# Reading the moving operand of every split product as two interleaved halves of its columns

## The reference

```python
z = h @ w_in[l]
u = causal_dwconv(h @ w_up[l], ffn_conv_w[l], ffn_conv_b[l])
x = x + (jax.nn.silu(gate) * val) @ w_down[l]
mix = (gate_a * y_a + gate_b * y_b) @ w_out[l]
gu = xb @ w_gu + b_gu
return ((up + 1.0) * glu) @ w_dn + b_dn
```

## Time and profile before

| what | value |
|---|---|
| median of three runs | 3237.35 us |
| the profiled execution's own time | 3235.76 us |
| its span, first to last instruction | 3233.9 us |
| TensorE matmul busy | 3073.2 us, 95% |
| VectorE, ScalarE, GpSimd busy | 59%, 53%, 23% |
| mean granted TensorE clock | 0.969 of full |
| DMA over the span | 677.48 MB, mean 209 GB/s |

### The profile page before, as it was taken

How to read it: one execution, slowest core, us unless ns; L and a number is a source line. 1 busy time by engine, 2 the same in 40 slices (tenths; PEclk the granted TensorE clock), 3 DMA queues, 4 the chain that set the end, 5 groups by cost and what they waited for, 6 DMA issues and landing times. The chain is left out here.

```text
span 3233.9 us, 40774 instructions
## 1 busy us (share of the span) xinstructions
PE 3073.2 (95%) x14356; PEld 2474.9 (77%) x14356; DVE 1923.7 (59%) x2190; ACT 1702.2 (53%) x2270; POOL 751.7 (23%) x409
## 2 busy tenths in 40 slices
PE   7988999998999999989999898999999999999987
PEld 6755778877877787768888776888888888888853
DVE  3247533343376604360032547999999999999973
ACT  4334534333566523332231425877887887887752
POOL 2400144442433243324444330000000000000020
PEclk9987999999999999989999998999999999999998
DMA  4236022222221222212222718999999999999960
GB/s 152 104 137 254 27 78 104 104 79 104 79 74 57 79 91 79 105 52 89 93 104 104 289 61 320 406 410 401 406 407 407 401 407 407 403 406 408 401 257 37
DMA packets 93434, 677.48 MB, mean 209 GB/s; under 512 B 10048, under 2 KB 10432, under 8 KB 32800
## 3 DMA queue, kind: packets, MB, share of 16 engines
q1 hardware_dynamic: 82320, 634.33, 50.2%
q0 software_dynamic: 6912, 25.17, 2.0%
q10 hardware_dynamic: 4112, 16.78, 1.3%
HBM read 637.97 MB, written 38.27 MB: 209 GB/s over the span
## 5 line engine op out<-in xcount | busy, mean ns | idle before, releaser
L143 POOL TENSOR_TENSOR ring_low<-ring,mix_ring_high 128x1024 fp32r<-128x1024 f32 x120 | 291.9, 2468 | 455.3 <-ACT mix_ring_high L138 455.3
L227 PE MATMUL psum<-mix_high,mix_ring_high 128*128 128x512 f32 x864 | 343.1, 397 | 13.1 <-DVE h_low L521 8.6
L229 PE MATMUL psum<-mix_high,ring_low 128*128 128x512 f32 x864 | 337.2, 390 | 0.0
L228 PE MATMUL psum<-h_low,mix_ring_high 128*128 128x512 f32 x736 | 287.4, 391 | 0.0
L143 POOL TENSOR_TENSOR ring_low<-ring,ff_ring_high 128x1024 fp32r<-128x1024 f32 x72 | 175.0, 2462 | 401.5 <-ACT ff_ring_high L138 224.6
L227 PE MATMUL psum<-ex_high,ex_rows_high 128*128 128x512 f32 x640 | 252.0, 394 | 1.2 <-DVE ring_low L2950 1.2
L229 PE MATMUL psum<-ex_high,ex_rows_low 128*128 128x512 f32 x640 | 249.3, 390 | 0.0
L2950 DVE TENSOR_TENSOR ring_low<-ring,ex_high 128x2048 fp32r<-128x2048 f32 x96 | 214.5, 2289 | 34.8 <-ACT ex_high L2777 34.4
L138 ACT ACTIVATE mix_ring_high<-ring 128x1024 fp32r<-128x1024 f32 x124 | 121.0, 1048 | 214.9 <-DMA ring<-wstream 214.9
L2950 DVE TENSOR_TENSOR ex_more_low<-ex_more,ex_high 128x2048 fp32r<-128x2048 f32 x96 | 217.0, 2288 | 0.0
L2950 DVE TENSOR_TENSOR ex_more_low<-ex_more,ex_high_in_x 128x2048 fp32r<-128x2048 f32 x96 | 216.9, 2287 | 0.0
(11 more groups left out here) (606 smaller groups left out, 7261.4 us busy)
## 6 DMA issues: line engine op xcount, KB each, us to landing
ex_more<-moe_w SPq DMA_DIRECT2D x256, 1024.0 KB, 7.8
ring<-wstream SPq DMA_DIRECT2D x87, 2048.0 KB, 8.3
ring<-moe_w SPq DMA_DIRECT2D x128, 1024.0 KB, 8.3
y_rows<-mx_zero ACTq DMA_DIRECT2D x1, 16384.0 KB, 50.5
ex_bias<-moe_b SPq DMA_DIRECT2D x32, 512.0 KB, 6.4
y_rows<-ex_y SPq DMA_DIRECT2D x32, 512.0 KB, 8.2
x<-xt SPq DMA_DIRECT2D x8, 256.0 KB, 5.3
rel<-rel_bias SPq DMA_DIRECT2D x1, 2048.0 KB, 9.5
```

The lines of the kernel that those rows point to most:

```text
L143: e.tensor_tensor(low, full, high.bitcast(F32), ALU.subtract).then_inc(self.low_ready, 1)
L227: pe.matmul(out, a[0], b[0], start=start, stop=False)
L228: pe.matmul(out, a[0], b[1], start=False, stop=False)
L229: return pe.matmul(out, a[1], b[0], start=False, stop=stop)
```

## The change

`split_product` takes `out` and both parts of `b` through a new helper, `two_halves`, before it issues the three products. The helper changes only the order in which the columns are named: of 512 columns it takes 0 and 1, then 256 and 257, then 2 and 3, then 258 and 259, and so on. The moving operand is read and the bank is written in that order, so each result lands where it did. The stationary operand `a` is not touched; no instruction, wait or transfer is added, removed or moved.

```diff
+def two_halves(t):
+
+    return t.rearrange("p (a b i) -> p b a i", a=2, i=2)
+
+
 def split_product(pe, out, a, b, start, stop):
 
+    out, b = two_halves(out), tuple(two_halves(t) for t in b)
     pe.matmul(out, a[0], b[0], start=start, stop=False)
     pe.matmul(out, a[0], b[1], start=False, stop=False)
     return pe.matmul(out, a[1], b[0], start=False, stop=stop)
```

## The result

The changed kernel takes 4421.19 us, the median of four runs from 4417.59 to 4432.46; the kernel before, in the same rounds, 3237.72 (3236.17 to 3243.23). The ratio is 1.3657, with a 95% interval from 1.3627 to 1.3687. The forecast was 3159 us, with a range from 3112 to 3300: the sign was wrong, and the range did not hold the time.

The account below looks back on a forecast made before the run. TensorE was taken to bound the kernel, with 11,376 split products at 226.7 ns each. Savings of 67 us outside the experts and 11 us in them, 78 us in total, gave 3159 us, range 3112 to 3300.

Parts of the forecast that it names:

- The counts and the price of a nanosecond: Split products in all stages: 6768 outside the experts, 4608 in them; one nanosecond per product is worth up to 11.4 us.
- the read of the moving operand: All split products: halves read at the weight load's pace lose most of the extra, 215.6 ns a product, 11 ns less.
- The clue: Plain split products: the extra 13.3 ns at full clock is absent at half clock, so no fixed number of TensorE's clocks.
- each change of place costs: Rival, all split products: 256 changes in read and write each cost time; 3388, 4450 or 5665 us; chance 0.25.
- The argument against it: All split products: the reads keep pairs, and one pair takes two clocks, enough to fetch the other half's.
- No change: Rival, all split products: the extra doesn't depend on the order, so 3237 us; chance 0.28.
- The write: PSUM write of all split products, in the same order by pairs: taken as costing nothing.
- the longer pattern: Address pattern in each split product's instruction: its greater length taken as costing nothing.
- half clock: Products just after a pause, clock granted at half: still 427 ns each after the change.
- The floor: Split products at full clock: 215.6 ns each, with 2.3 ns over the columns taken from the plain float32 products.
- The experts' limit: Expert stage: DMA engines at share 0.99 make the next weights late, so 11 us gained, bounds 0 and 51.
- faster in the experts too: Rival, expert stage: DMA engines carry 4.9% more, all of the 51 us is gained, 3119 us; chance 0.03.

Follow-up runs that it names:

- even and odd pairs: Changed kernel, all split products, with all even pairs of columns first, then all odd pairs, instead of halves in turn: 5759.72 us.
- halves by fours: Changed kernel, all split products, with the two halves in turn four columns at a time instead of two: 3491.11 us, ratio 1.0774.
- four places: Changed kernel, all split products, with pairs of columns from four quarters in turn instead of two halves: 5668.93 us.
- changed write: Experts' call alone writes the bank as interleaved halves and reads the moving operand in plain order, other ten calls plain: 3239.45 us, kernel before 3238.52.
- half lines: Experts alone read the even pairs of the moving operand's columns, each pair twice in a row: 3237.87 us, kernel before 3237.12.
- 64 lines: Experts alone read the moving operand's first 256 columns in groups of four, each group twice in a row: 3227.31 us, kernel before 3237.12.
- halves by sixteens: Changed kernel with sixteen columns at a time: 3380.40 us, kernel before 3239.64; with the experts' weights shifted as well, 3382.26 and 3382.41 us.
- even and odd fours: Changed kernel, all split products, with all even groups of four columns first, then all odd ones: 3300.61 us.

## Why the prediction was wrong, point by point

**The counts and the price of a nanosecond held.** 11,376 products, up to 11.4 us a nanosecond: 105.2 ns came to 1196.7 us. TensorE has no cover in any stage, as the rivals' part said, so the loss arrived in full, in the experts too.

**The step that failed is the read of the moving operand.** From 240 ns beside one small tile and 231 ns at 72 columns it concluded that most of the extra 13.3 ns is the two reads getting into each other's way, and that halves at the load's pace would lose it. Measured in its place: plain products are limited by 128 lines of 16 bytes at 1.77 ns each (453.3 ns with 256 fetches, 215.8 with 64), and the new order makes every line be visited twice with another line between. The rows it rested on were real but small: the place of the weights is worth 6 ns on top of the line limit and, in the places tried, nothing below it. That the 240 and 231 ns are the same effect is likely, but no run shows it. And the bounds were drawn too narrow: 213.3 to 226.7 ns on the main path came from rows that all read straight on, which can't bound a read that doesn't.

**The clue that was misread.** The prediction noted that the extra is no fixed number of TensorE's clocks. That was right, and it already pointed at a supply with a price in nanoseconds: 128 lines take 227 ns, more than the columns' 213 at full clock and far less than their 427 at half.

**The rival "each change of place costs"** had the sign and, by one of its prices, the size: one clock a change, 107 ns, 4450 us, against 107 to 113 ns and 4421 us. Its reason does not hold, though. It isn't the write (free), and it isn't the change as such: seven changes cost nothing, and even and odd pairs double the time although they jump back only once. At one clock a change the halves by fours (127 changes) would have taken 280 ns and the four places (as many changes as two) 333; measured were 250.8 and 442.5. That one clock came out fits this one order only. Four places in turn, with three other lines between two visits, cost nearly 256 fetches. Why it is 333 ns with one line between stays open: (333.3 - 226.7)/1.77 = 60, as if some 60 of the 128 second visits fetched again; but if each second visit only held up the fetching for 0.83 ns, 128 x (1.77 + 0.83) would be 333 as well. Both are worked out, and no run tells them apart. The argument against it, that a pair gives two clocks to fetch the other half's, was wrong: a fetch takes 1.77 ns, four clocks at 0.417 ns and a little more. The two statements of the Trainium skill (Advanced Engine Details and Errata, Memory Cachelines) that the rival quoted are on PSUM. The run with the changed write decides between them for this order: with two consecutive elements in a row a product took 227.5 ns.

**No change** fell with the first distance.

**The write, the longer pattern and half clock** were right: 227.5 ns with the changed write, 227.5 with the pattern of half lines, 426 ns at half clock.

**The floor** was right as well, though the change never got there: 215.6 ns was taken from the float32 products, and 215.8 was measured with 64 lines. **The experts' limit** was right in size: 11 us was allowed there and 9.8 was gained, not the 50 that the rival *faster in the experts too* had. That is one run on each side, and the runs of the kernel before alone spread over 12.7 us. Its reason, late weights, is not shown: TensorE then waits for VectorE's rows of activations, and the DMA share was 1.00 before as well.

**What would show it wrong** named this case: more than 227 ns in all stages alike.

## What to carry to other kernels

A moving operand of 4-byte elements that is read straight on is here limited by the lines fetched from SBUF (226.7 ns for 128), not by its columns (215.8): keep all four columns of a 16-byte line together, and don't come back to a line after another one, which cost 333 to 453 ns. Permute on the side of the PSUM write, where pairs were free (227.5 ns), or by runs of 64 columns (227.5 ns). And when a change alters how something is read, rows that all read the old way bound nothing: let the range reach to the price that one fetch a visit would have.

## What the runs showed of the hardware that was not expected

- The price of a line hardly follows TensorE's clock: 256 fetches took 453 ns at full and 453 to 466 at half clock.
- Stationary tiles 32, 64, 128 or 384 bytes off a multiple of 512 cost 6 ns a product, 256 bytes off none, but with halves by sixteens (240.0 ns) the weights' place no longer matters.
- Halves in turn by runs of 4 to 32 columns cost 10 to 24 ns although every line is fetched once; by 64 columns they cost nothing. Why, why even and odd fours cost 6.6 ns, and why some tensors show 328 or 340 instead of 333 ns in the changed kernel, stays open.
